# Eighteen matmuls without a reader leave the tails of the hybrid and the sliding-window attention

## The reference

```python
x = first_block(x, ...)    # differential attention, RWKV-7 time mix, memory attention, 16-expert MoE
return second_block(x, ...)

def second_block(x, ...):  # two layers
    h = h + 0.5 * swiglu(rmsnorm(h, g[0]), ...)
    u = rmsnorm(h, g[1])
    # layer 0: hybrid mixer = dilated attention, 8 heads, and top-k attention, 8 heads
    # layer 1: sliding-window attention, 16 heads, 2 key heads, a learned sink for each head
    h = h + mix
    h = h + 0.5 * swiglu(rmsnorm(h, g[2]), ...)
```

```python
s = einsum('nbqhgd,nbshd->nbhgqs', qb, kw) * dh ** -0.5 + bias
p = exp(where(mask, s, -inf) - m)
o = einsum('nbhgqs,nbshd->nbqhgd', p, vw) / sum(p)
```

## Time and profile before

| | |
|---|---|
| median of 3 runs | 1586.2 us |
| the runs | 1583.1, 1586.2, 1587.89 us |
| the profiled execution's own time | 1588.31 us |
| its span, first to last instruction | 1586.5 us |
| mean granted clock of TensorE | 0.98 of full speed |
| TensorE matmuls busy | 1519.1 us, 9232 matmuls |
| VectorE busy | 1177.7 us |
| ScalarE busy | 815.0 us |
| time that DMA packets take, share of 16 engines (largest queue) | 54.3% |

### The profile page before, as it was taken

One profiled execution on the slowest core, in us unless ns is written; L12 is line 12 of the kernel. 1 busy time (PEld: TensorE's weight loads), 2 busy tenths in 40 slices (PEclk: granted clock), 3 DMA queues, 4 the chain that ended last, 5 costly groups with the idle time before them and its releaser, 6 DMA issues.

```text
span 1586.5 us, 27289 instructions
## 1 busy us (share of the span) xinstructions
PE 1519.1 (96%) x9232; PEld 1340.3 (84%) x9232; DVE 1177.7 (74%) x1830; ACT 815.0 (51%) x1302; POOL 49.6 (3%) x59
## 2 busy tenths in 40 slices
PE   6999888999999999999999999999999999999997
PEld 6888777898888978888898888888888888888886
DVE  5865665889798978777757677777877774677776
ACT  6523554777677764344544654434434445553342
POOL 1030000000000000000000200000000000000000
PEclk9999799999999999999999999999999999999999
DMA  7312241899799967655542455665655542365552
GB/s 268 120 40 67 82 149 42 301 350 330 291 332 351 341 249 250 189 184 185 163 154 81 153 191 187 198 186 172 199 180 190 186 159 80 120 199 191 182 186 76
DMA packets 82150, 299.69 MB, mean 189 GB/s; under 512 B 9278, under 2 KB 9406, under 8 KB 81952
## 3 DMA queue, kind: packets, MB, share of 16 engines
q1 hardware_dynamic: 79632, 289.97, 54.3%
q0 software_dynamic: 2160, 8.66, 1.7%
q10 hardware_dynamic: 288, 0.12, 0.0%
HBM read 297.59 MB, written 1.11 MB: 188 GB/s over the span
## 4 chain that ended last, share of the span: by engine, by line
PE 86%; DVE 8%; ACT 3%; issue 1%; DMA 1%; DVEq 0%; POOL 0%; SPq 0%; POOLq 0%; ACTq 0%
PE ps L2051 18%; PE ps L1785 15%; PE ps L1787 15%; PE ps L1786 15%; PE ps L2049 10%; PE ps L2048 3%; PE ps L1791 2%; DVE w_lo L1094 2%; PE ps L1993 1%; PE ps L1961 1%; ACT w_hi L637 1%; DMA raw<-in_wstream 1%; DVE xT L1152 1%; PE ps L2239 1%; PE ps L2069 1%
## 5 line engine op out<-in xcount | busy, mean ns | idle before, releaser
L1094 DVE TENSOR_TENSOR w_lo<-raw,w_hi 128x1024 fp32r<-128x1024 f32 x549 | 654.4, 1222 | 175.9 <-ACT w_hi L637 174.2
L637 ACT ACTIVATE w_hi<-raw 128x1024 fp32r<-128x1024 f32 x549 | 551.0, 1055 | 293.5 <-PE ps L1787 249.9
L2051 PE MATMUL ps<-xT,w_hi 128*128 128x512 f32 x1232 | 439.1, 396 | 0.0
L2049 PE MATMUL ps<-xT,w_lo 128*128 128x256 f32 x1408 | 364.8, 279 | 0.0
L1785 PE MATMUL ps<-w_hi,xT 128*128 128x256 f32 (+2 forms) x864 | 268.8, 311 | 9.6 <-DVE w_lo L1094 7.0
L2049 PEld LDWEIGHTS ps<-xT,w_lo 128*128 128x128 f32 x1408 | 265.3, 188 | 14.3
L2051 PEld LDWEIGHTS ps<-xT,w_hi 128*128 128x128 f32 x1232 | 231.2, 188 | 47.6
L1787 PE MATMUL ps<-w_hi,xT 128*128 128x256 f32 (+2 forms) x864 | 258.5, 299 | 0.0
L1786 PE MATMUL ps<-w_lo,xT 128*128 128x256 f32 (+2 forms) x864 | 258.0, 299 | 0.0
L1785 PE MATMUL ps<-w_hi,h_hi 128*128 128x512 f32 x480 | 188.2, 392 | 4.4 <-DVE h_lo L1337 4.4
L1785 PEld LDWEIGHTS ps<-w_hi,xT 128*128 128x128 f32 x864 | 166.3, 193 | 28.4 <-issue 23.2
(11 more groups left out here) (339 smaller groups left out, 1637.9 us busy)
## 6 DMA issues: line engine op xcount, KB each, us to landing
raw<-in_wstream SPq DMA_DIRECT2D x549, 512.0 KB, 4.7
arena<-bias_rows POOLq DMA_DIRECT2D x2, 2048.0 KB, 13.4
const<-in_const POOLq DMA_DIRECT2D x1, 1112.0 KB, 7.6
x_res<-in_x SPq DMA_DIRECT2D x2, 512.0 KB, 4.4
arena<-in_mem POOLq DMA_DIRECT2D x1, 1024.0 KB, 6.4
out<-arena SPq DMA_DIRECT2D x2, 512.0 KB, 2.7
smallw<-in_smallw POOLq DMA_DIRECT2D x1, 768.0 KB, 4.6
prow<-in_prow POOLq DMA_DIRECT2D x1, 512.0 KB, 5.2
```

What stands on the lines that cost most here:

```text
L637: nc.scalar.activation(w_hi[:, slot, lo:hi], raw[:, slot, lo:hi], ACT.Copy).then_inc(S_(f"hi_{part_}"), 1)
L1094: tt(w_lo[:, slot, lo:hi], raw[:, slot, lo:hi], w_hi[:, slot, lo:hi].bitcast(F32), ALU.subtract).then_inc(S_(f"lo_{part_}"), 1)
L2049: low = mm(bank[:, 0:S], w_lo[:, s, c:c + P], xT_hi[:, k, :], start=False, stop=False)
L2051: last = mm(bank, w_hi[:, s, c:c + P], both, start=False, stop=k == KD - 1)
```

## The change

In `trans_unit` the call of `keep_busy` goes, and its condition with it. `woven(u) > 6` held for the units 7 to 15 of the hybrid attention and the same of the sliding-window attention, 18 matmuls in all.

```diff
@@ -1967,8 +1967,6 @@
                 da = un["kind"] == "da"
                 if u:
                     pe.wait_ge(S_("att_pt"), u if inside(u) and woven(u) or u <= DA_UNITS else u - 1)
-                if woven(u) > 6:
-                    keep_busy(ps[:, trans_bank(u), :], 1)
                 pe.wait_ge(S_("att_comb" if da else "att_exp"), u + 1)
                 for m in range(1 if da else 2):
                     for kb in range(un["nk"]):
```

## The result

| | before | changed |
|---|---|---|
| median, same chip | 1585.87 us (14 runs) | 1588.47 us (14 runs) |
| the runs | 1583.1 to 1587.89 | 1583.93 to 1592.69 |
| ratio, 95% interval | | 1.002, 1.0011 to 1.003 |
| profiled execution, span | 1588.31, 1586.5 us | 1588.51, 1586.7 us |
| TensorE matmuls | 9232 | 9214 |

A forecast was written before the change was run, and what follows sets the result against it. TensorE holds 86% of the chain, but the prediction took VectorE's gapless work in the tails to turn most savings into waits. 0.6 + 0.1 = 0.7 us off the median 1586.2 gave 1585.5 us; range 1582.5 to 1589.5.

The forecast's parts named there:

- The price of 0.29 us: TensorE time freed per removed matmul, 0.34 less 0.05 us; 18 give 5.2 us as upper bound.
- Hybrid tail, 0.6 us: Saving forecast for the hybrid attention's tail, between 0 (all of it waits) and 2.6 us (none of it).
- 0.4 forecast: Hybrid tail: product of unit 11 starts earlier, putting the last scores at 886.7 instead of 887.12 us.
- the last transposes: Hybrid tail: they start some 0.05 us after the last exponentials without the ninth unread matmul, another 0.15 us off.
- 5.7 or 0.2 less: Sign of being right: hybrid tail, start of unit 11's product to that of the last takes 5.7 us or 0.2 less.
- Sliding-window tail, 0.1 us: Only the ninth removal counts: last transposes start at 1361.9 instead of 1362.00 us; between 0 and 2.6 us.
- I expect 2.4 GHz to hold: Both tails: TensorE stays over 80% busy except around 1356 us, so its clock does not fall.
- Rival 2: Clock falls within the tails: one to three low stretches, 1587.0 to 1590.0 us, chance 0.19; four or more, slower, 0.07.
- two or three low stretches: Allowance in the range for the clock falling in the tails; one stretch of 3.4 us was priced at 1.5 us.
- The gap behind the tail: Behind the last product, with and without the change; low clock on the 16 transposes there costs under 1 us.
- The rule of the Trainium skill: Tails with a third of their steps transposes could lose the clock, up to 1599 us; the prediction set it aside.

The follow-up runs named there:

- e14: Repeat of e6: the change, but with the unread matmuls of units 11 and 12 of the sliding-window tail kept; +2.7 us, ratio 1.0014 against the kernel before.
- e6: Of the 18 unread matmuls in the kernel before, only those beside units 11 and 12 of the sliding-window tail stay; +4.5 us, ratio 1.0017.
- e7: Of the 18 unread matmuls in the kernel before, only the sliding-window tail's units 7 to 10 and 13 to 15 stay; +5.0 us, ratio 1.0028.
- e9: The changed kernel with VectorE's third split moved behind the maximum of unit 15 in the sliding-window tail only; -1.3 us, ratio 0.9998 against the kernel before.
- e10: The changed kernel with VectorE's third split moved behind the maximum of unit 15 in both tails; -3.0 us, ratio 0.9984 against the kernel before.
- e13: The changed kernel run again, unaltered; +2.9 us, ratio 1.0022 against the kernel before.
- e1: The kernel before with the nine unread matmuls taken out of the hybrid tail only; -0.3 us, ratio 1.000.
- e15: e10 plus four unread matmuls in the gap behind each tail's last product; -2.4 us, ratio 0.9985 against the kernel before.
- e11: The kernel before, all unread matmuls kept, with VectorE's third split moved behind the maximum of unit 15 in both tails; -0.8 us, ratio 0.9993.
- e12: e11 plus four unread matmuls in the gap behind each tail's last product; -3.1 us, ratio 0.999 against the kernel before.
- e3: The kernel before with all 18 unread matmuls kept in place but writing 64 columns instead of 512; +4.2 us, ratio 1.0023.

## Why the prediction was wrong

- **The price of 0.29 us** held. Where nothing waits, two steps of the changed kernel take 3.24 us (873.10 to 876.34, scores of units 9 and 11), and two of the kernel before 3.80 (1345.99 to 1349.79): 0.28 for each removal.
- **Hybrid tail, 0.6 us:** 0.38 was measured. Up to the product of unit 11 the tail won 0.45 us (0.4 forecast). Two terms were off. The product of unit 11 takes 1.04 us to the last scores (883.13 to 884.17), not 0.93, and so gives 0.11 back. And the last transposes brought 0.06 us instead of 0.15: they start at 887.60, 0.14 us behind the last exponentials (887.46), where it was 0.20 before and 0.05 was assumed. From the product of unit 11 to the last one it takes 5.79 us; 5.7 or 0.2 less was forecast.
- **Sliding-window tail, 0.1 us:** right as long as the clock held. 10.07 against 10.08 us up to unit 14, and D of e14, where seven of this tail's nine are gone, is 19.70 against 19.69. So the 0.1 us for the last transposes did not show there either; their wait for the exponentials is 0.41 us long.
- **The clock: here the prediction failed.** The step was "I expect 2.4 GHz to hold", from two stretches and a count of work in the tail as a whole. The stretch at 208 us has packed steps and no waits, and an unread matmul stands right ahead of it (207.31). The one at 1330 us has projection matmuls of 256 columns in its busy time. Neither is like a tail of attention steps alone whose removed work turns into waits at one spot. (The one at 1330 us is idle for 2.2 of 5 us, no less than the spot where the clock fell. So idle time alone doesn't decide; that the projection matmuls make the difference is not tested.) The prediction had that very wait in hand (0.51 us at 1356.07) and booked its growth as free, since VectorE held the time. It was free in time and not in clock: 1.08 us with 0.52 ahead and 0.51 behind it, and TensorE fell to 1.2 GHz in both profiles. The mean over 16 us said 80% busy; from 1350 to 1354.2 us these three waits are 2.1 us, half of the stretch. That the waits there and what fills them matter is shown by e6, e14 and e7 (filled at units 11 and 12 or not) and by e9 and e10 (the long wait removed).
- **Rival 2** is what happened, with 0.19 given to the size measured. That the median still lies between 1582.5 and 1589.5 is due to the two or three low stretches allowed for, not to the forecast, which had the time go down. Rival 2's price was too high in one part: 1.5 us for 3.4 us at low clock. The change had 13.7 us of it, from 1354.6, for 3.1 us in D and 0.5 in E, so 0.9 us for each 3.4. Part of the slower work takes the place of a wait: in e13, with 6.8 us of it, D grew by 1.66 us, 0.8 for each 3.4.
- **The gap behind the tail** was put at under 1 us, "with and without the change". B differs by 0.73 us (2.59 to 3.32), as said. But in these profiles it goes with the change (9 of 9 against 1 of 4), and the 1.25 us in C were not foreseen at all. In e1's profile these, and 0.66 us behind E, outweigh the 0.38 us won in the hybrid tail; that they do so in its other executions is not shown.
- **The rule of the Trainium skill** ("TensorE: Matmul & The Clock Gate", Part 4: transposes do not count as activity in the way matmuls do) was set aside because 16 transposes were followed by a rise. That is again so in the changed kernel (1365.47 for 3.31 us, 1.00 from 1368.3). But from 1358 to 1362 us scores, transposes and products keep TensorE busy for 4.00 of 4 us at 0.50 without a rise, while in e13 such a mix got it back at about 1361. These runs neither show the rule nor refute it. Its warning pointed the right way, but nothing here shows that it did so for the right reason.

## What to carry to other kernels

A matmul that nobody reads can be worth its place where TensorE waits for another engine: taken out of the sliding-window tail, nine of them saved no time up to unit 14 and lengthened the waits. Judge the clock at the spot where the waits grow, not by a mean over the stage, and look behind the stage too. One can also remove the cause of a wait instead of filling it: with one 1.2 us split of VectorE moved behind the last maximum of each tail, the clock held in them without any unread matmul, and the kernel came out ahead of the one before (e10, 0.9984 with an interval of 0.9971 to 0.9996, some 2.5 us; e15 agrees). That this beats moving the split and keeping the unread matmuls (e11, e12) is not shown.

## What was not expected of the hardware

- Work of the same kind held the high clock in one place and did not bring it back in another. Scores, transposes and products ran at 1.00 in e10 from 1350 to 1358 us, with TensorE busy for 3.49 and 3.23 of each 4 us, and at 0.50 in the changed kernel from 1358 to 1362, with TensorE busy throughout. In e13 the clock did come back amid such work, at 1361.1.
- 1.14 us of waiting for a maximum did not decide by itself: with the unread matmuls of 512 columns on either side of it the clock held (e6, e14), with ones of 64 columns it fell (e3), and without them it fell at a wait of only 0.80 us (e7).
- One changed tail gives different executions: the low part lasted 13.7 us in one profile and 6.8 in the other. The times roughly follow the mean clock, from 1583.93 us at 0.983 to 1592.69 at 0.975 over 14 runs of the changed kernel. Such a spread, 8.8 us, is no mark of the change, though: the kernel before has 4.8 us in 14 runs on the same chip, but 6.4 to 11.0 in 29 to 35 runs on the four others.
